# Partial products of high and low parts gathered in one set of PSUM columns, in a two-block transformer kernel

## The reference, cut to what matters

```python
# layer 0 ("even"): chunked attention with 8 heads (A) and differential attention (B)
proj = rmsnorm(x) @ even_w_in            # 2048 -> 6144
x = x + concat(attention_a, attention_b) @ even_w_out
x = x + (silu(h @ w_gate) * (h @ w_up)) @ w_down
# layer 1 ("odd"): indexed sparse attention over a latent of 256, 16 heads
proj = rmsnorm(x) @ odd_w_in             # queries, latent, index queries and keys
x = x + attention(q, c_lat, w_uk, w_uv) @ odd_w_out
x = x + (silu(h @ w_gate) * (h @ w_up)) @ w_down
x = rmsnorm(x)
# second block
proj = x @ w_in + b_in                   # c_val, c_glu, c_gate, q, k, v, a_gate
y_conv = silu(layer_norm(conv31(c_val * sigmoid(c_glu)) + conv_b)) * silu(c_gate)
y_attn = window_attention(q, k, v, sinks) * silu(a_gate)
y = concat(y_conv, y_attn) @ w_out + b_out
return layer_norm(2 ** 0.25 * x + y)
```

## Time and profile before

| | |
|---|---|
| median of 3 runs (lowest to highest) | 2674.64 us (2672.57 to 2680.85) |
| profiled execution: time | 2678.86 us |
| profiled execution: span | 2677.0 us |
| mean granted TensorE clock over the span | 0.976 of full speed |
| PE, DVE, ACT, POOL busy | 2551.8, 1543.9, 1221.7, 120.4 us |
| share of the span | 95, 58, 46, 4 % |
| DMA | 462.12 MB, mean 173 GB/s |

### The profile page before, as it was taken

The page is one execution under the profiler, slowest core; times in us unless marked ns, Lnnn a source line. Parts: engine busy times, 40 slices in busy tenths (PEclk is TensorE's granted clock), DMA queues, the critical chain, the costliest instruction groups (busy, mean ns, idle before and its releaser), DMA issues.

```text
span 2677.0 us, 37397 instructions
## 1 busy us (share of the span) xinstructions
PE 2551.8 (95%) x13231; PEld 2178.3 (81%) x13231; DVE 1543.9 (58%) x2083; ACT 1221.7 (46%) x1544; POOL 120.4 (4%) x104
## 2 busy tenths in 40 slices
PE   7999989999999999999999999999999997999876
PEld 5888868888888888887887888888888886888765
DVE  6555556444444555556765554545454445999855
ACT  5444445444444444445454544444444444545543
POOL 2000001000000000000221000000000001000100
PEclk9999989999999999999998999999999998999988
DMA  6444435655656555555444555556555554554433
GB/s 202 157 154 157 156 119 185 191 189 187 191 187 191 187 188 187 187 171 177 150 142 146 188 190 191 188 188 188 189 187 189 189 189 138 174 176 148 172 111 110
DMA packets 372045, 462.12 MB, mean 173 GB/s; under 512 B 16639, under 2 KB 278961, under 8 KB 371562
## 3 DMA queue, kind: packets, MB, share of 16 engines
q1 hardware_dynamic: 369792, 453.63, 52.7%
q0 software_dynamic: 1536, 7.06, 0.8%
q10 hardware_dynamic: 618, 0.09, 0.0%
HBM read 458.58 MB, written 2.14 MB: 172 GB/s over the span
## 4 chain that ended last, share of the span: by engine, by line
PE 59%; issue 28%; DVE 9%; ACT 2%; POOL 1%; ACTq 0%; DVEq 0%; POOLq 0%
PE PG L226 20%; PE PG L259 18%; PE PG L229 10%; PE PG L244 4%; DVE ws L207 2%; PE PG L247 2%; DVE cacc L1490 2%; PE PO L922 1%; PE PS L859 1%; POOL acc L632 1%; ACT ws L201 1%; PE PS L902 1%; DVE ts L895 0%; PE PS L798 0%; PE PS L860 0%
## 5 line engine op out<-in xcount | busy, mean ns | idle before, releaser
L207 DVE TENSOR_TENSOR ws<-raw,ws 128x1024 fp32r<-128x1024 f32 x860 | 1060.1, 1234 | 929.2 <-ACT ws L201 924.2
L201 ACT ACTIVATE ws<-raw 128x1024 fp32r<-128x1024 f32 x860 | 909.9, 1059 | 1133.6 <-PE PG L226 537.7
L259 PE MATMUL PG<-ws,hs 128*128 128x512 f32 x4224 | 964.0, 390 | 0.0
L259 PEld LDWEIGHTS PG<-ws,hs 128*128 128x128 f32 x4224 | 791.4, 188 | 163.4
L226 PE MATMUL PG<-hs,ws 128*128 128x512 f32 x1536 | 554.6, 403 | 33.3 <-DVE vst L1075 14.1
L226 PE MATMUL PG<-fs,ws 128*128 128x512 f32 x1408 | 491.0, 395 | 0.0
L229 PE MATMUL PG<-hs,ws 128*128 128x256 f32 x1536 | 437.5, 290 | 2.2 <-DVE ws L207 2.1
L229 PE MATMUL PG<-fs,ws 128*128 128x256 f32 x1408 | 390.7, 279 | 0.0
L226 PEld LDWEIGHTS PG<-hs,ws 128*128 128x128 f32 x1536 | 294.2, 193 | 98.4 <-issue 26.0
L226 PEld LDWEIGHTS PG<-fs,ws 128*128 128x128 f32 x1408 | 263.5, 188 | 61.1
L229 PEld LDWEIGHTS PG<-hs,ws 128*128 128x128 f32 x1536 | 298.3, 194 | 7.5 <-DVE ws L207 3.0
(11 more groups left out here) (283 smaller groups left out, 1504.4 us busy)
## 6 DMA issues: line engine op xcount, KB each, us to landing
raw<-in_w_gate SPq DMA_DIRECT2D x176, 512.0 KB, 4.2
raw<-in_w_up SPq DMA_DIRECT2D x176, 512.0 KB, 3.5
raw<-in_w_down SPq DMA_DIRECT2D x176, 512.0 KB, 3.2
raw<-in_even_w_in SPq DMA_DIRECT2D x96, 512.0 KB, 3.8
raw<-in_w_in SPq DMA_DIRECT2D x84, 512.0 KB, 3.6
raw<-in_odd_w_in SPq DMA_DIRECT2D x44, 512.0 KB, 3.5
raw<-in_even_w_out SPq DMA_DIRECT2D x32, 512.0 KB, 3.2
raw<-in_odd_w_out SPq DMA_DIRECT2D x32, 512.0 KB, 3.2
```

The costliest lines, as they stand in the source:

```text
L201: e.activation(ws[j % RING][:, :, 0, :], raw[:, j % RING], ACT.Copy).then_inc(s_hi, 1)
L207: e.tensor_tensor(w[:, :, 1, :], raw[:, j % RING], w[:, :, 0, :].bitcast(F32), ALU.subtract).then_inc(s_lo, 1)
L259: ins = e.matmul(out[:, b, :], x_, w[:, kk, :, h, :], start=first and kk == 0 and n == 0, stop=last and kk == 1 and n == 2)
```

## The change

`mul_T` and `mul_N` issue three products of 256 columns for each pair (high by high, high by low, low by high), all added into the same columns 0:256. A group's result is then a quarter of `PG`, two banks with one half in each, and groups alternate between banks 0 and 2 in every stage. `crossing` and `load_drain_copy` are gone. A drain is one operation that reads PSUM: on DVE where it scales by the norm or adds to the residual, on ACT where it adds a bias (`with_bias`). The loops of the stages A and Bs are unrolled and have 12 groups each, so the values' group no longer shares its buffer with the next iteration's queries. In the stage U keys are drained by ACT and DVE side by side. SO uses `mul_W`: 512 output columns a group, units of two k-tiles, two iterations of two groups of eight units, and a new order of the first 16 units.

```diff
-    PG = nc.alloc_psum_tensor("PG", [P, 2, 2, 512], F32)
+    PG = nc.alloc_psum_tensor("PG", [P, 4, 512], F32)
...
-    def mul_T(e, buf, j, k0, rhs, first, last, tiles=(0, 1)):
+    def mul_T(e, bank, j, k0, rhs, first, last, tiles=(0, 1)):
         w = ws[j % RING]
         for kk in range(UK):
             for c in tiles:
                 wh, wl = (w[:, kk, h, c * P:(c + 1) * P] for h in (0, 1))
-                st, sp = first and kk == 0, last and kk == UK - 1
-                r = rhs[:, k0 + kk, :, :].rearrange("p a s -> p (a s)")
-
-                def big():
-                    return e.matmul(PG[:, buf, c, :], wh, r, start=st, stop=sp)
-
-                def less():
-                    return e.matmul(PG[:, buf, c, 0:S], wl, rhs[:, k0 + kk, 0, :], start=False, stop=False)
-                for f in ((big, less) if st else (less, big)):
-                    ins = f()
+                xh, xl = (rhs[:, k0 + kk, h, :] for h in (0, 1))
+                for n, (w_, x_) in enumerate(((wh, xh), (wh, xl), (wl, xh))):
+                    ins = e.matmul(PG[:, bank + c, 0:S], w_, x_, start=first and kk == 0 and n == 0,
+                                   stop=last and kk == UK - 1 and n == 2)
         return ins
-    def mul_N(e, j, k0, lhs, first, last, out, cols=slice(0, UC)):
+    def mul_N(e, bank, j, k0, lhs, first, last):
 
         w = ws[j % RING]
         for kk in range(UK):
             for b in (0, 1):
-                hh, hl = (lhs[:, k0 + kk, h, b * P:(b + 1) * P] for h in (0, 1))
-                st, sp = first and kk == 0, last and kk == UK - 1
-
-                def big():
-                    return e.matmul(out(b)[:, 0:2 * n], hh, w[:, kk, :, cols], start=st, stop=sp)
-
-                def less():
-                    return e.matmul(out(b)[:, 0:n], hl, w[:, kk, 0, cols], start=False, stop=False)
-                for f in ((big, less) if st else (less, big)):
-                    ins = f()
+                xh, xl = (lhs[:, k0 + kk, h, b * P:(b + 1) * P] for h in (0, 1))
+                for n, (x_, h) in enumerate(((xh, 0), (xh, 1), (xl, 0))):
+                    ins = e.matmul(PG[:, bank + b, 0:UC], x_, w[:, kk, h, :], start=first and kk == 0 and n == 0,
+                                   stop=last and kk == UK - 1 and n == 2)
...
-            e.wait_ge(s_drain, seg.group(i, k) - seg.dist[k] + 3)
+            e.wait_ge(s_drain, seg.group(i, k) + 1)
...
-    def crossing(e, seg, i, k, func=ACT.Identity, scale=1.0, bias=0.0, part=slice(0, 2), mm=True):
-
-        e.wait_ge(s_mm, seg.end(i, k) + RING)
-        b = seg.bufs[k]
-        return e.activation(cross[:, b, part, :], PG[:, b, part, S:2 * S], func, scale=scale, bias=bias)
-
...
-    gA = Seg(4, [4, 4, 4], [0, 1, 0], [1, 3, 2], 2)
-    gBs = Seg(4, [4, 4, 4], [0, 1, 0], [1, 3, 2], 2)
...
-    gEO = Seg(4, [4, 4], [1, 0], [2, 2])
...
-    gSO = Seg(4, [4, 4], [0, 1], [2, 2])
...
+    def halves(seg, k, m=2):
+
+        return PG[:, seg.banks[k]:seg.banks[k] + m, 0:S]
+
+    gA = Seg(1, [4] * 12, [0, 2] * 6)
+    gBs = Seg(1, [4] * 12, [0, 2] * 6)
+    gEO = Seg(4, [4, 4], [0, 2])
...
+    gI = Seg(1, [4] * 4, [0, 2, 0, 2])
+    gU = Seg(2, [1] * 4, [0, 0, 2, 0])
...
+    gSO = Seg(2, [8, 8], [2, 0])
...
-    def load_drain_copy(e, seg, i, k, dst, p_scale=None):
-
-        b = seg.bufs[k]
-        e.wait_ge(s_cross, seg.group(i, k) + 1)
-        if p_scale is None:
-            return e.tensor_tensor(dst, PG[:, b, :, 0:S], cross[:, b], ALU.add)
-        return e.scalar_tensor_tensor(dst, PG[:, b, :, 0:S], p_scale, cross[:, b], ALU.mult, ALU.add)
...
     def scaled_drain(e, seg, i, k, dst, scale=1.0, turned=None):
 
-        b, m = seg.bufs[k], dst.shape[1]
-        done = seg.sb + seg.scaled * i + k + 1
-        e.wait_ge(s_cross, seg.group(i, k) + 1)
-        c = cross[:, b, 0:m]
-        e.tensor_tensor(c, PG[:, b, 0:m, 0:S], c, ALU.add).then_inc(sem("summed"), 1)
-        e.wait_ge(sem("summed"), done)
+        m = dst.shape[1]
+        e.wait_ge(s_mm, seg.end(i, k) + RING)
+        c = halves(seg, k, m)
...
                     def drain(i):
-                        load_drain_copy(e, seg, i, k, cross[:, b]).then_inc(sem(p + "sum"), 1)
-                        w(e, p + "sum", g + 1)
+                        e.wait_ge(s_mm, seg.end(i, k) + RING)
                         xx = x[:, bass.ds(g * 2, 2), :]
-                        e.tensor_tensor(xx, xx, cross[:, b], ALU.add).then_inc(s_drain, 1)
+                        e.tensor_tensor(xx, xx, halves(seg, k), ALU.add).then_inc(s_drain, 1)
...
-                                e.wait_ge(s_cross, seg.group(i, k) + 1)
-                                w(e, "rnT", 2)
-                                for b in (0, 1):
-                                    c = seg.bufs[k]
-                                    ins = e.scalar_tensor_tensor(vst[:, b, :], PG[:, c, b, 0:S], rnT[:, b:b + 1], cross[:, c, b, :], ALU.mult, ALU.add)
+                                    ins = e.tensor_scalar(vst[:, b, :], halves(seg, g)[:, b, :], rnT[:, b:b + 1], None, ALU.mult)
...
-                    c = slice(t * P, (t + 1) * P)
-                    big = lambda: e.matmul(PG4[:, h, :], wk[:, h, 0, c], cs[:, t].rearrange("p a s -> p (a s)"), start=t == 0, stop=t == 1)
-                    less = lambda: e.matmul(PG4[:, h, 0:S], wk[:, h, 1, c], cs[:, t, 0, :], start=False, stop=False)
-                    for f in ((big, less) if t == 0 else (less, big)):
-                        ins = f()
+                    wh, wl = (wk[:, h, m, t * P:(t + 1) * P] for m in (0, 1))
+                    xh, xl = (cs[:, t, m, :] for m in (0, 1))
+                    for n, (w_, x_) in enumerate(((wh, xh), (wh, xl), (wl, xh))):
+                        ins = e.matmul(PG[:, bank + h // 2, (h % 2) * S:(h % 2 + 1) * S], w_, x_, start=t == 0 and n == 0, stop=t == 1 and n == 2)
...
-                        e.activation(cross4[:], PG4[:, :, S:2 * S], ACT.Copy).then_inc(s_cross, 1)
+                        e.activation(kC[:, bass.ds(8 * i + 4 * (k // 2), 2), :], key_pair(gU.banks[k]), ACT.Copy).then_inc(s_cross, 1)
...
                     if k % 2 == 0:
-                        e.tensor_tensor(kC[:, bass.ds(8 * i + 4 * (k // 2), 4), :], PG4[:, :, 0:S], cross4[:], ALU.add).then_inc(s_drain, 1)
+                        e.tensor_copy(kC[:, bass.ds(8 * i + 4 * (k // 2) + 2, 2), :], key_pair(gU.banks[k] + 1)).then_inc(sem("ud"), 1)
                     else:
-                        e.tensor_copy(vC[:, 0, bass.ds(1024 * i + 512 * (k // 2), 512)], PO[:, 0, :]).then_inc(s_drain, 1)
+                        e.tensor_copy(vC[:, 0, bass.ds(1024 * i + 512 * (k // 2), 512)], PO[:, 0, :]).then_inc(sem("ud"), 1)
+                    w(e, "ud", 4 * i + k + 1)
+                    e.wait_ge(s_cross, 11 + 4 * i + k + 1)
+                    e.sem_inc(s_drain, 1)
...
-    def bias_cross(e, seg, i, k, tile, **kw):
-
+    def with_bias(e, seg, i, k, dst, tile, func=ACT.Identity, scale=1.0, b=None):
+
+        e.wait_ge(s_mm, seg.end(i, k) + RING)
+        e.wait_ge(s_drain, seg.group(i, k) + 2)
         for t in (0, 1):
-            ins = crossing(e, seg, i, k, part=slice(t, t + 1), bias=bin2[:, bass.ds(tile + t, 1)], **kw)
-        ins.then_inc(s_cross, 1)
+            ins = e.activation(dst[:, t, :], halves(seg, k)[:, t, :], func, scale=scale, bias=(bin2 if b is None else b)[:, bass.ds(tile + t, 1)])
+        return ins
...
                         def drain(i):
                             if k == 0:
-                                load_drain_copy(e, gCv, i, 0, hc[:, 2 * i:2 * i + 2, CONV_W - 1:]).then_inc(s_drain, 1)
+                                w(e, "p2", 4)
+                                with_bias(e, gCv, i, 0, hc[:, 2 * i:2 * i + 2, CONV_W - 1:], 2 * i).then_inc(s_drain, 1)
                             else:
-                                load_drain_copy(e, gCv, i, 1, cross[:, gCv.bufs[1]]).then_inc(s_drain, 1)
-                        group_side(e, gCv, i, k, lo, drain, conv_hooks(e, i - 1 if i else None, k))
+                                w(e, "hc", i)
+                                with_bias(e, gCv, i, 1, kst, 8 + 2 * i, ACT.Sigmoid).then_inc(s_drain, 1)
...
-                            bias_cross(e, gQ2, i, k, 24 + 2 * g)
+                            w(e, "bq", 1)
+                            with_bias(e, gQ2, i, k, qall[:, 2 * g:2 * g + 2, :], 2 * g, scale=SCALE2, b=bq).then_inc(s_drain, 1)
...
-    order = (2, 3, 0, 1)
-    turns = ((0, 2), (0, 3), (1, 2), (1, 3), (0, 0), (1, 0), (0, 1), (1, 1))
-    last_of = {6: 0, 7: 1}
...
+    order = (4, 5, 6, 7, 0, 1, 2, 3)
+    turns = [(k, n) for k in (0, 1) for n in range(4)] + [(k, n) for m in (4, 6) for k in (0, 1) for n in (m, m + 1)]
+    last_of = {13: 0, 15: 1}
+
+    def so_first(i, j):
+        return turns[j] if i == 0 else divmod(j, 8)
...
+            def add_dve(k, end):
+                e.wait_ge(s_mm, end + RING)
+                g, q = 2 * i + k, gSO.banks[k]
```

(17 more changed lines are left out.)

188 lines of the change are left out of this document (79 added, 109 removed).

## The result

The changed kernel takes 2656.98 us (median of 4 runs, 2654.67 to 2657.41) beside 2674.27 us for the kernel before on the same chip (2672.57 to 2680.85): ratio 0.9929, 95% interval 0.9911 to 0.9947. So the change brings 17 to 22 us; 11.4 were forecast, and the measured time lies inside the stated range, 6 us under the likeliest value.

What follows compares the result with a forecast made beforehand. TensorE (PE) was taken to bound the kernel, busy 2551.8 of 2677.0 us. The terms 42 - 23 - 9.5 - 20.4 - 0.5 sum to -11.4 us, from 2674.64 to 2663, range 2644 to 2690.

Steps and rivals of the forecast that it cites:

- The bound: Whole kernel: TensorE (PE) is busy 2551.8 of 2677.0 us; only product price and 125 us of PE standing move the time.
- Three short products for a pair: 3744 pairs become three 256-column products: 360 ns instead of 348.7 each, +42 us.
- The weakest number: Price of one 256-column product, 120 ns, taken as a difference of two steps; 1 ns of it is 11 us.
- all of it lies on the path: The short products' +42 us counts in full, because PE ends these stages.
- Bank order: Even stage: alternating banks remove seven PE waits on vst (some 15.3 us) and half clock after five: -23 us.
- One-operation drains: Shorter drains count only where PE waits for the result (norms, qi, kst, kraw, vC, ts): -9.5 us.
- The last product: Final stage in 512-column form and new unit order: -20.4 us, and -0.5 us for the operations behind it.
- The replay: Last product rebuilt step by step: one 4.4 us wait, 24 units left at 2568.5, end at 2633.8 instead of 2654.2.
- B: Rival: short products lock into the slow rhythm, 123.2 ns or more, making the kernel slower at 2699; chance 0.17.
- half-way case: Rival: only 3 in 10 short-product groups run in the slow rhythm, +11 us, 2674; chance 0.10.
- C: Rival: the last product's second wait stays, some 7 us of the 20.4 lost, 2670 to 2674; chance 0.10.
- D: Rival: short products cost 116 ns, giving 2618, or 2630 by the Trainium skill's rule; chance 0.10.

Runs made afterwards that it cites:

- e12_copy_in_drain: Changed kernel, with DVE first copying the result from PSUM and then adding it in output and down projections (two operations per drain): 2656.25 us, ratio 0.9922.
- e1_three_products: Kernel before, with each 512-and-256-column pair made three 256-column products (the key product's pairs stay), drains unchanged: 2710.43 us, ratio 1.0124.
- e5: Changed kernel without the one-operation drains (copy and add stay; the key product's 32 pairs stay pairs): 2666.86 us, ratio 0.9963.
- e4_both_parts: Kernel before with the edits of e2_alternating and e3_last_product together, no short products or one-operation drains: 2629.48 us, ratio 0.9825.
- e2_alternating: Kernel before, with the two even stages unrolled into 12 groups each and their buffers alternating: 2651.3 us, ratio 0.9903.
- e3_last_product: Kernel before, with only the last product as in the changed kernel (512 columns a group, new unit order): 2656.32 us, ratio 0.9927.
- e9_plain_order: Changed kernel, with the first 16 units of the last product in plain order, eight of each group: 2666.95 us, ratio 0.9964.
- e8_one_step_where_waited: e4_both_parts with the changed kernel's short products and one-operation drains only in stage I and for stage U's keys: 2625.56 us, ratio 0.9808.
- e11_128_columns: Changed kernel, with each 256-column product in both down projections cut into two of 128: 3092.29 us, ratio 1.1551.
- e10_other_weights_each: Changed kernel, with the three transposed products reordered so that no two neighbours share the stationary part: 2655.79 us, ratio 0.9919.

## Why the prediction was right

**The bound** was read rightly. PE ends every stage, DVE's and ACT's savings show only where PE waits, and e12_copy_in_drain shows the rest of it directly.

**Three short products for a pair**, forecast +42. The weakest number, 120 ns, is 120.0 in the steady down-projection groups of every kernel with short products. The two down projections pay 7.63 us each, 10.8 ns a pair (11.3 was the average over all stages; with every second group slow, 10.1 was to be expected there, and the first group pays more). Measured alone it is +33 (e1_three_products) or +37 (e5 against e4_both_parts). The step that failed a little is "all of it lies on the path": in the stages with waits, a part of it is taken out of the waits (2.5 us on `ts` and `vst`); some 2 to 6 us more are missing without a shown cause.

**Bank order**, forecast -23: measured -26 alone (e2_alternating). The row's waits and the half clock behind them were the right two terms (3 us of the gain are neither, see above), and the second was counted for the right reason: PE ran at 1.2 GHz after a wait, and without the wait it doesn't.

**One-operation drains**, forecast -9.5: measured -11.7. That the number is close is in part luck. The waits that the term lists shrink by 5.7 us and not 9.5: `vC` by 0.4 instead of 1.3, the norms by 0.8 instead of 1.3 each, `kst` by 0.4 instead of 0.8. On `ts` the drains take 0.5 instead of 2; the other 1.9 had already gone with the short products (e1_three_products). Some 5 us of less half clock in stages I, U and Q, which the term left out, make up for it.

**The last product**, forecast -20.4 and -0.5: measured -20.5 in the stage and -21.1 in the time (e3_last_product). The replay, made from the rows of before, hit each of its stations within 0.15 us. The tail lost 1.2 us and not 0.5. e9_plain_order shows that one item of it, four more units that PE can run ahead of the second wait, is worth half of the gain.

**The sum.** Measured parts: 37 - 26 - 11.7 - 21 = -22, where the changed kernel measures -17 to -22. Of this only the adding up of the second and the fourth is a test (47.2 for 48, e4_both_parts); the first and the third are the steps from there to the changed kernel and close the sum by the way they were taken. The forecast's -11.4 has the same four terms, the first three off in the same direction, by 5, 3 and 2 us. One omission lies across them: PE at half clock. What the products in half-clock stretches take beyond their full-speed price, added up over the whole trace, is some 26 us before and 12 after. The prediction took the 7.5 us behind the waits on `vst`, and the last product's share stands in its replay; it left out the rest, above all the 2.3 us in stage I, where the clock stayed up in that execution.

The stated range doesn't quite follow from its own terms: 118 ns a product gives 2641, not 2644, and two thirds of the way to B give 2687, not 2690. The measured time lies inside either.

**The rivals.** B (slow rhythm for short products) and its half-way case fell: one rhythm of 120.0. C fell: the second wait is gone (0.52 us before unit 8). D fell: 120.0, not 116. By the Trainium skill ("TensorE: Matmul & The Clock Gate", Back-to-back issue gap) N/2.4 + 2.5 would be 109.2 ns for 256 columns and 55.8 for 128. The same section of the Trainium skill calls this the gap of an isolated product; for a stream with a load ahead of each product it gives 131 ns at 512 columns and 81 at 128. The runs of this kernel, with fp32r weights loaded for every product, show 226.7 at 512, 120.0 at 256 and 111.7 at 128, and the measurement decides.

**What the forecast didn't ask** is which parts of a change belong together. The change costs 33 to 37 us with its short products and gives them back with the one-operation drains only to a third. The other two edits, which don't need them, bring 47. e4_both_parts and e8_one_step_where_waited are the kernels that follow from that.

## What to carry to other kernels

Price each part of a bundle by itself; here the headline part (fewer partial results, shorter drains) was a net loss of some 25 us that two unrelated edits covered. One long and one short product are cheaper than three short ones as long as the price of a product has a part that doesn't shrink with its columns, and a drain is worth shortening only in those groups behind which the bounding engine waits. A wait that gets shorter can also spare a stretch of half clock, which may be worth as much as the wait. When an engine waits for one half of its input, the order of its independent work is worth as much as the chain that it waits for.

## What the runs showed of the hardware

- **Width and price of an fp32r product.** From start to start in a steady stream: 226.7 ns for 512 columns, 120.0 for 256, 111.7 for 128. From 256 to 128 columns only 8 ns go, so the last one looks like a floor (e11_128_columns). Whether the neighbour has the same stationary part makes no difference, and a load is counted for each product either way (e10_other_weights_each).

- **The scatter between executions goes with the granted clock.** The eight executions of the kernel before in the last comparison, in order of mean granted clock:

```
clock   span, us
0.974   2679.0, 2678.3
0.975   2675.8
0.976   2674.6, 2673.9
0.977   2675.6, 2673.0
0.978   2672.6
```

The code is the same, and so is the work. In the two comparisons before it the order is looser, with the same slope: 1.3 to 1.5 us for each 0.001 of the clock. In the traces single stretches of 3.41 us at half clock come or stay away at the same place. The changed kernel and e9_plain_order have the same code up to the last product, and in stages I and U (window of PE, the page's columns) they read:

```profile
1186.00:1270.00 84.00, 77.91 (x552) 0.99 0.61 185
```

```profile
1186.00:1270.00 84.00, 77.92 (x545) 0.98 0.60 183
```

The first is the changed kernel, the second e9_plain_order. The stretch that only the second has:

```profile
1225.04:1228.45 3.41, 3.41 (x17) 0.50 0.56 157
```

Stage I takes 49.2 us in the first and 50.7 in the second. A stretch costs 1.5 us, which is more than several terms of the forecast, so a single trace can't carry a difference of that size; this holds for the differences between stages above, too.

- **The two rhythms of the long and short pair** (346.8 and 353.1 ns) don't depend on which of the two goes first, and equal products show one rhythm. The cause of the two stays open. The slow one costs some 9 us in the kernel before and 7 in e4_both_parts, an estimate from the share of units that run at it and 6.3 ns a pair.
